# First MLP of a fused two-block kernel: its up projection as seven block products per pair of feature tiles, in chunks of 512 middle features

## What is computed

```python
def sq_relu_mlp(h, w1, w2):
    return jnp.square(jax.nn.relu(h @ w1)) @ w2
...
h_lat = h_lat + ml[5] * sq_relu_mlp(modulate(rms_norm(h_lat, norm2_w[layer]), ml[3], ml[4]), mlp_w1[layer], mlp_w2[layer])
if need_ctx:
    h_ctx = h_ctx + mc[5] * sq_relu_mlp(modulate(rms_norm(h_ctx, norm2_w[layer]), mc[3], mc[4]), mlp_w1[layer], mlp_w2[layer])
```

## Time and profile before

| | |
|---|---|
| median of 3 runs | 2884.98 us (2881.59 to 2889.40) |
| profiled execution | span 2890.5 us; the page gives no other time for it |
| TensorE busy | 2746.6 us, 95% of the span, 21852 products |
| VectorE, ScalarE, POOL busy | 1152.2 us (40%), 921.4 us (32%), 400.6 us (14%) |
| mean granted TensorE clock | 0.982 |

### The profile page before, as it was taken

One profiled execution on the slowest core, in us unless ns is written; L12 is line 12 of the kernel. 1 busy time (PEld: TensorE's weight loads), 2 busy tenths in 40 slices (PEclk: granted clock), 3 DMA queues, 4 the chain that ended last, 5 costly groups with the idle time before them and its releaser, 6 DMA issues. The chain is left out here.

```text
span 2890.5 us, 50817 instructions
## 1 busy us (share of the span) xinstructions
PE 2746.6 (95%) x21852; PEld 2073.4 (72%) x21852; DVE 1152.2 (40%) x1696; ACT 921.4 (32%) x1523; POOL 400.6 (14%) x329
## 2 busy tenths in 40 slices
PE   8987989999999999899999999999997888999999
PEld 6764654444445885667888888887786777788887
DVE  3225442323323416644433323234354554544333
ACT  4234331111112224255331212223374545432322
POOL 0014120000000402353100000010004564100001
PEclk9999999999999999999999999999999999999999
DMA  6537819999995112100111211211210000223231
GB/s 252 204 120 278 310 59 372 417 410 418 414 412 204 46 51 61 34 30 30 59 59 58 73 58 62 69 58 59 91 37 31 4 4 33 88 88 98 91 102 58
DMA packets 160787, 390.40 MB, mean 135 GB/s; under 512 B 17007, under 2 KB 108042, under 8 KB 147818
## 3 DMA queue, kind: packets, MB, share of 16 engines
q1 hardware_dynamic: 148378, 199.19, 20.4%
q10 hardware_dynamic: 12240, 188.75, 15.6%
HBM read 381.36 MB, written 5.77 MB: 134 GB/s over the span
## 5 line engine op out<-in xcount | busy, mean ns | idle before, releaser
L2175 PE MATMUL ps<-mlp_h_low,mlp_w_high 128*128 128x512 f32 (+1 forms) x768 | 272.0, 354 | 0.0
L2175 PE MATMUL ps<-mlp_h_high,mlp_w_high 128*128 128x512 f32 (+1 forms) x768 | 271.9, 354 | 0.0
L2175 PE MATMUL ps<-mlp_h_high,mlp_w_low 128*128 128x512 f32 (+1 forms) x768 | 271.6, 354 | 0.0
L2028 ACT ACTIVATE mlp_w_high<-mlp_ring 128x2048 fp32r<-128x2048 f32 x64 | 122.2, 1912 | 316.2 <-PE ps L2175 316.2
L2175 PE MATMUL ps<-mlp_x_low,mlp_w_high 128*128 128x512 f32 (+1 forms) x576 | 204.0, 354 | 0.0
L2175 PE MATMUL ps<-mlp_x_high,mlp_w_high 128*128 128x512 f32 (+1 forms) x576 | 203.9, 354 | 0.0
L2175 PE MATMUL ps<-mlp_x_high,mlp_w_low 128*128 128x512 f32 (+1 forms) x576 | 203.7, 354 | 0.0
L260 POOL TENSOR_TENSOR aT<-aT 128x512 f32<-128x512 f32 (+1 forms) x25 | 52.1, 2084 | 1000.7 <-ACT aT L252 1000.1
L2032 DVE TENSOR_TENSOR mlp_w_low<-mlp_ring,mlp_w_high 128x2048 fp32r<-128x2048 f32 x64 | 146.6, 2292 | 62.8 <-ACT mlp_w_high L2028 62.8
L2244 DVE SCALAR_TENSOR_TENSOR hT<-ps,mod,hT 128x512 f32<-128x512 f32 x96 | 63.5, 662 | 256.0 <-PE ps L2175 256.0
L2175 PEld LDWEIGHTS ps<-mlp_h_high,mlp_w_high 128*128 128x128 f32 x768 | 145.2, 189 | 20.5
(11 more groups left out here) (566 smaller groups left out, 5942.7 us busy)
## 6 DMA issues: line engine op xcount, KB each, us to landing
mlp_ring<-in_mlp_w_dram SPq DMA_DIRECT2D x64, 1024.0 KB, 5.3
e_wg<-in_w_gate_dram ACTq DMA_DIRECT2D x15, 4096.0 KB, 16.2
e_wu<-in_w_up_dram ACTq DMA_DIRECT2D x15, 4096.0 KB, 15.1
ring<-in_w_down_dram ACTq DMA_DIRECT2D x15, 4096.0 KB, 13.2
ring<-in_ada_w_dram SPq DMA_DIRECT2D x16, 2048.0 KB, 8.8
h_rest<-in_ada_w_dram SPq DMA_DIRECT2D x8, 2048.0 KB, 8.2
ring<-in_w_in_dram SPq DMA_DIRECT2D x6, 2048.0 KB, 10.6
proj_ring<-in_even_w_in_dram SPq DMA_DIRECT2D x8, 1024.0 KB, 5.1
```

Source lines behind the costliest of these rows:

```text
L2028: act.activation(self.high[:, slot], self.ring[:, slot], ACT.Copy).then_inc(self.w_high, 1)
L2175: last = pe.matmul(bank(st, n, s, b - a), w[:, st % 2, k, n * P:(n + 1) * P], x[:, k, a:b], start=(k == 0 and p == 0), stop=(k == KT - 1 a ...
```

## The change

The first MLP gets its own function, `mlp_by_blocks`; the second keeps `mlp`. The middle features go in 8 chunks of 512. Up: a chunk has two panels (u = 0, 1) of 256 columns. A panel's weights form a 2 x 2 arrangement of blocks (4 feature tiles x 128 columns), the normed activations one of (4 feature tiles x 384 tokens). In place of the eight block products come seven (Winograd's form of Strassen's scheme): e = 0 to 6, each of 4 feature tiles x 3 parts of 384 columns. Three of their weight operands are raw blocks and four are sums of blocks, made by POOL for each panel (`combine`: 4 instructions of 512 elements). The activation operands are made once, in the opening: shift on ScalarE (L2145, now without rounding), differences on POOL (`beside`: `first`, then lines L2215 and L2220, six instructions of 768 elements) and VectorE (`second`), and seven high and low parts in two halves each (L2152, L2179).

The results: c11 = p1 + p2 (e = 0, 2 in one bank), c12 = p1 + p6 + (p5 + e3), c22 = p1 + p6 + p5 + p7, c21 = p1 + p6 + (p7 + e6), where p1, p5, p7, p6 are e = 0, 1, 4, 5. Since later products are added onto a bank, ScalarE first copies p1, p5 and p7 out (`snapshot`), and products e = 2, 3, 6 wait for that (`copied`). VectorE makes the sums, squares with Relu in one instruction, and the low parts. Down: 4 steps of 256 output features over 4 middle tiles, in units of 384 tokens.

The diff, cut:

```diff
-    def add(self, pool):
+    def add(self, pool, between=None):
         total = self.sum_of(self.E, self.T)
         for n in range(1, KT - 2):
+            if between and n == 4:
+                between(pool)
...
+                squares.add(pool, then.get("pool") if then else None)
...
+class ProductParts:
...
+    SUM_AT = {1: 0, 5: 1, 4: 2, 3: 3}
...
+    def combine(self, pool, c, u):
+        z = 2 * c + u
+        first, second, third, fourth = (self.sums[:, i] for i in range(4))
+        pool.wait_ge(self.loaded[u], 16 * (2 * c + 1))
+        pool.tensor_tensor(first, self.block(u, 1, 0), self.block(u, 1, 1), ALU.add).then_inc(self.summed, 1)
+        pool.wait_ge(self.summed, 4 * z + 1)
+        pool.tensor_tensor(second, first, self.block(u, 0, 0), ALU.subtract).then_inc(self.summed, 1)
+        pool.wait_ge(self.summed, 4 * z + 2)
+        pool.tensor_tensor(fourth, self.block(u, 0, 1), second, ALU.subtract).then_inc(self.summed, 1)
+        pool.tensor_tensor(third, self.block(u, 0, 0), self.block(u, 1, 0), ALU.subtract).then_inc(self.summed, 1)
...
+class NormedBlocks(Normed):
...
+    def source(self, e, k):
+        return (self.at(k, 0), self.first[:, k:k + 2], self.at(4 + k, 0), self.at(4 + k, 1), self.at(k, 1), self.second[:, k:k + 2],
+                self.at(4 + k, 0))[e]
+    def highs(self, act):
...
+        def high(e, j):
+            if e in (0, 2, 3):
+                act.wait_ge(self.shifted, 2 * (2 * j + 2 + (4 if e else 0)))
+            else:
+                act.wait_ge({1: self.t1, 4: self.t3, 5: self.t2, 6: self.t4}[e], j + 1)
+            act.activation(self.high[:, e, 2 * j:2 * j + 2], self.source(e, 2 * j), ACT.Copy).then_inc(self.x_high, 1)
+        shift(0)
+        shift(1)
+        high(0, 0)
+        shift(2)
+        shift(3)
+        high(0, 1)
+        shift(4)
+        high(1, 0)
+        shift(5)
+        high(1, 1)
+        shift(6)
+        shift(7)
+        for e in range(2, 7):
+            for j in range(2):
+                high(e, j)
+    def lows(self, dve):
...
+        def low(e, j):
+            dve.wait_ge(self.x_high, 2 * e + j + 1)
+            dve.tensor_tensor(self.low[:, e, 2 * j:2 * j + 2], self.source(e, 2 * j), self.high[:, e, 2 * j:2 * j + 2].bitcast(FP),
+                              ALU.subtract).then_inc(self.x_low, 1)
+        def second(j):
+            dve.wait_ge(self.t1, j + 1)
+            dve.wait_ge(self.shifted, 2 * (2 * j + 6))
+            dve.tensor_tensor(self.second[:, 2 * j:2 * j + 2], self.at(4 + 2 * j, 1), self.first[:, 2 * j:2 * j + 2], ALU.subtract)\
+                .then_inc(self.t2, 1)
+        dve.wait_ge(self.rooted, 2)
+        for k in range(4):
+            scale(k)
+        low(0, 0)
+        scale(4)
+        scale(5)
+        low(0, 1)
+        scale(6)
+        low(1, 0)
+        scale(7)
+        low(1, 1)
+        low(2, 0)
+        second(0)
+        low(2, 1)
+        second(1)
+        for e in range(3, 7):
+            for j in range(2):
+                low(e, j)
+    def beside(self, pool):
+        for j in range(2):
+            k = 2 * j
+            pool.wait_ge(self.shifted, 2 * (k + 2))
+            pool.tensor_tensor(self.first[:, k:k + 2], self.at(k, 1), self.at(k, 0), ALU.subtract).then_inc(self.t1, 1)
+        for j in range(2):
+            k = 2 * j
+            pool.wait_ge(self.t1, j + 1)
+            pool.wait_ge(self.shifted, 2 * (k + 6))
+            pool.tensor_tensor(self.at(k, 1), self.at(4 + k, 1), self.at(k, 1), ALU.subtract).then_inc(self.t3, 1)
+        for j in range(2):
+            k = 2 * j
+            pool.wait_ge(self.t2, j + 1)
+            pool.wait_ge(self.x_low, 4 + j + 1)
+            pool.tensor_tensor(self.at(4 + k, 0), self.at(4 + k, 0), self.second[:, k:k + 2], ALU.subtract).then_inc(self.t4, 1)
...
+        BANK_OF = (0, 3, 0, 3, 2, 1, 2)
...
+                with pe.Fori(0, C) as c:
+                    for u in range(2):
+                        pe.wait_ge(added, 24 * c + 18 + 6 * u)
+                        for e in range(7):
+                            pe.wait_ge(W.w_low, 18 * c + 7 * u + e + 1)
+                            if e in (2, 3, 6):
+                                pe.wait_ge(copied, 4 * (2 * c + u) + {2: 1, 3: 2, 6: 4}[e])
+                            wh, wl = W.up_part(W.high, e), W.up_part(W.low, e)
+                            for k in range(4):
+                                if u == 0 and k % 2 == 0:
+                                    pe.wait_ge(x_low, 2 * e + k // 2 + 1)
+                                for i, (w, x) in enumerate(((wh, xh), (wh, xl), (wl, xh))):
+                                    last = pe.matmul(bank(u, BANK_OF[e]), w[:, k], x[:, e, k], start=(e in (0, 1, 4, 5) and k == 0 and i == 0),
+                                                     stop=(k == 3 and i == 2), skip_group_check=True)
+                            last.then_inc(full, 1)
+                    for dn in range(4):
+                        wh, wl = W.down_part(W.high, dn), W.down_part(W.low, dn)
+                        pe.wait_ge(W.w_low, 18 * c + 14 + dn + 1)
+                        if dn < 2:
+                            pe.wait_ge(made, 4 * (2 * c + dn + 1))
+                        else:
+                            pe.wait_ge(added, 24 * c + 24 + 6 * (dn - 1))
+                        for q, (n, half) in enumerate(DOWN):
+                            for k in range(4):
+                                if dn == 0 and q == 0:
+                                    pe.wait_ge(h_low, 8 * c + (3, 4, 6, 7)[k])
+                                if dn == 0 and q == 2 and k == 3:
+                                    pe.wait_ge(h_low, 8 * c + 8)
+                                for i, (w, x) in enumerate(((wh, hh), (wh, hl), (wl, hh))):
+                                    last = pe.matmul(bank(dn % 2, q), w[:, k, n * P:(n + 1) * P], x[:, k, HALF * half:HALF * half + HALF],
+                                                     start=(k == 0 and i == 0), stop=(k == 3 and i == 2))
+                            last.then_inc(full, 1)
...
+                def snapshot(c, u, e, name):
+                    act.wait_ge(full, 30 * c + 7 * u + e + 1)
+                    if name == "p1":
+                        act.wait_ge(normed.t1, 2)
+                    act.activation(place(u, name), bank(u, BANK_OF[e]), ACT.Copy).then_inc(copied, 1)
+                def hidden(c, u, name, i):
+                    act.wait_ge(made, 4 * (2 * c + u) + i + 1)
+                    act.activation(h_at(hh, u, name), place(u, name), ACT.Copy).then_inc(h_high, 1)
+                def steps(c, more):
+                    for u in range(2):
+                        def weight(e):
+                            if u == 0:
+                                act.wait_ge(full, 30 * c + e + 1)
+                                W.up_high(act, c, 1, e)
+                            elif e in (0, 2, 4):
+                                act.wait_ge(full, 30 * c + 7 + e + 1)
+                                W.down_high(act, c, e // 2)
+                        snapshot(c, u, 0, "p1")
+                        weight(0)
+                        snapshot(c, u, 1, "p5")
+                        weight(1)
+                        snapshot(c, u, 2, "c11")
+                        weight(2)
+                        weight(3)
+                        hidden(c, u, "c11", 0)
+                        snapshot(c, u, 4, "p7")
+                        weight(4)
+                        weight(5)
+                        hidden(c, u, "c12", 1)
+                        hidden(c, u, "c22", 2)
+                        weight(6)
+                        hidden(c, u, "c21", 3)
+                    act.wait_ge(full, 30 * c + 14)
+                    W.down_high(act, c, 3)
...
+                        weight(0)
+                        weight(1)
+                        weight(2)
+                        dve.wait_ge(copied, 4 * z + 3)
+                        square("c11")
+                        weight(3)
+                        hidden("c11", 0)
+                        dve.wait_ge(copied, 4 * z + 4)
+                        dve.tensor_tensor(place(u, "p5"), place(u, "p5"), place(u, "p7"), ALU.add).then_inc(joined, 1)
+                        weight(4)
+                        products(5)
+                        dve.tensor_tensor(place(u, "p1"), place(u, "p1"), bank(u, 1), ALU.add).then_inc(joined, 1)
+                        weight(5)
+                        dve.wait_ge(joined, 2 * z + 2)
+                        dve.tensor_tensor(place(u, "c12"), place(u, "p1"), bank(u, 3), ALU.add).then_inc(pre, 1)
+                        dve.tensor_tensor(place(u, "c22"), place(u, "p1"), place(u, "p5"), ALU.add).then_inc(pre, 1)
+                        dve.wait_ge(pre, 3 * z + 1)
+                        square("c12")
+                        dve.wait_ge(pre, 3 * z + 2)
+                        square("c22")
+                        hidden("c12", 1)
```

(18 more changed lines are left out.)

## The result

The changed kernel takes **2924.55 us** (2921.19 to 2930.08, 4 runs) beside 2886.39 us (2881.59 to 2889.40) for the kernel before: ratio 1.0141, 95% interval 1.0113 to 1.0168, slower. The forecast was 2894, the range ended at 2908.

A forecast was written before the change was run, and what follows sets the result against it. It took TensorE's columns alone to bound the first MLP; -33.4 (fewer products) + 25.6 (opening) + 1.7 (clock) + 15 (chunk ends) + 0.7 - 0.6 gave +9.0 on 2885.0, so 2894 us, range 2869 to 2908.

The forecast's parts named there:

- Part 1: First MLP's up products: 1344 instructions of 384 columns for 1536, 192 fewer at 0.1738 us, -33.4 us.
- Part 2: MLP opening: TensorE's third product waits for the whole chain until about 1462 instead of 1436.4, +25.6 us.
- So the two engines' work adds: Opening: POOL and VectorE do not run beside each other, so 8.5 + 13.9 + 10.8 = 33.2 us.
- the lower bound: Opening, if POOL is let in early: third product at 1456.5, a loss of +20 us.
- part 3: Clock after the opening's long wait: 0.50 for 3.4 us, +1.7 us (0 to 3.4).
- whatever parts are ready: Opening: products 3 to 14 wait for the copy behind all high parts, the last needing POOL's sixth difference.
- Part 4: End of each chunk's up part: TensorE stalls 1.9 us a chunk for the low part, +15 us in all.
- VectorE's gap for ScalarE: Chunk ends: VectorE's wait for ScalarE's high part lets in one POOL sum of 1.27 us, +1.2 us.
- The bound of 2.5 a chunk: Upper bound of the chunk-end stall: 8 x 2.5 = 20 us.
- the other waits are met: Chunks: waits for `copied` before products 3, 4 and 7, `w_low` and `added` cost nothing.
- Rival 2: POOL gets its turn at every VectorE instruction end: opening -4, chunks +28, 2918 us; chance 0.11.
- the other way to this sum: Chunk ends: each stall lowers the clock for 3.4 us, 8 x 1.7 = +14 us.

The follow-up runs named there:

- experiment 5: Changed kernel with ScalarE copying the first two banks after the high parts of x's third and fourth form: ratio 1.0156 to the kernel before.
- experiment 6: Changed kernel with earlier copies of the opening's first two banks and fifth product, and POOL's second-unit sums after x's last low: ratio 1.0142 to the kernel before.
- experiment 1: Changed kernel with POOL's sums for the next chunk waiting for the 18th low part: ratio 1.0024 to the kernel before.
- experiment 9: Changed kernel with late POOL sums, first two down tiles ahead, and the second unit's first-bank copy before c21's high part: 0.9973 of the kernel before, 2874.24 us.

## Why the prediction was wrong

- **Part 1** held: 173.5 ns where 173.8 were forecast; -35 for -33.4.
- **Part 2**, +25.6: the size held (+25), by luck, for the composition did not. "So the two engines' work adds" gave the third product 33.2 us after the first scaling; it came at 27.9, within 0.2 us of the lower bound, because POOL got its turns. The rest came back behind it, in two more waits and in half pace, for which part 3 had only +1.7. That the copy behind all high parts decides ("whatever parts are ready") was half the story: experiments 5 and 6 took it away and met the next of the same kind twice.
- **Part 4** is the step that failed: +15 for +33. It failed in the overlap of POOL and VectorE. Its chain without POOL, 1.0 us of stall, was right, as experiment 1 shows with 0.9. Its price for POOL, one sum of 1.27 us let in by "VectorE's gap for ScalarE", was not: three to four sums, each at the end of a VectorE instruction, 2.5 to 3.9 us more. The bound of 2.5 a chunk lay under the 3.4 to 4.8 that seven of the eight chunks lost there. That the other waits are met did not hold for the second unit's third product, which waited for its copy in seven chunks, 3 us; experiment 9 took that away.
- **Part 3** failed with it: one stretch at 0.50 was forecast, there was one behind every long chunk end, 17 us, and two in the opening. Rival 2 named both mechanisms, but as "the other way to this sum", when they add: the stall causes the low clock. Added up it would have said +47, 9 too many where the forecast was 29 too few. That its +33 came near is in part luck: it had some 43 us for the chunk ends' gaps, 33 were there, and it had nothing for the half pace behind them, which made up for it.
- **The evidence.** The order of the two engines rested on the earlier trace rows. That row, of the trace before, is the only POOL operation with more than six ends of VectorE instructions inside it (it has 14), and it has an operand spread from one element. The sums and differences of this change read two full rows, as do L2861 (up to 2602 ns) and L2859 (3.28 us), which show POOL held for an instruction or two and no more. The Trainium skill, "SBUF — State Buffer", Who interferes with whom, says that a VectorE instruction with two SBUF inputs and a GpSimd instruction that reads SBUF exclude each other, and that the order of issue decides who is held; 0.5 us instructions that become 1.6 in turn with sums of 1.3 to 1.6 us agree; the 8.07 us with 14 VectorE instructions inside them do not, and there the measurement stands. Rival 2, which is that rule, should have had far more than 0.11.
- **Smaller slips.** The range "by the bounds of parts 1 to 4" started at 2884, but their lower ends add up to 2877 at most. In the earlier trace rows POOL's operation ends 1.6 us after VectorE's scan, not 1.8. Neither bears on the miss.

## What to carry to other kernels

Before work is put on POOL, ask what VectorE does in the same microseconds: here each POOL operation on two SBUF rows put its whole length into VectorE's chain, once per VectorE instruction, and a transfer's landing picked the moment. Either make POOL wait until the chain is through, or give TensorE work that does not need the chain; each alone gave back over 30 us here. Price a stall of 3 to 4 us on TensorE with the low clock behind it (17.3 us for seven here, 2.5 each). In an opening, follow the chain behind a copy before you move it: one at a time only moved the wait, and all of them in a new order gave 1.2 us by the trace, up to 5.6 by the medians.

## What was not expected of the hardware

- POOL's operation of 256 elements beside VectorE's unbroken row of instructions: 8.07 us where its second operand is one element per partition, 1.05 us where it is a full row.
- Granted clock: 0.50 for 3.4 or 6.8 us behind each of the chunk ends with a gap of 3.0 to 4.1 us, none behind gaps of 1.07 us (eight in experiment 1). Between the two it was not sharp: in experiment 6 one gap of 1.93 us, with one of 1.10 behind it, was followed by 3.4 us at 0.50 (10 us from 1760 on: 0.83), while in experiment 5 one of 3.0 us, with the same behind it, was not (from 1694 on: 1.00). With sixteen products of no use in the gap it stayed at 1.00 in six of seven.
- Raising the clock did not pay where another engine sets the pace: 0.77 to 0.90 over the opening, with a stretch of 525.8 us for 525.6.
